# Modulation rows summed in PSUM banks, spread over two up groups and six down stages, and twelve more seven-product tiles

## What is computed

```
c_act = silu(c)
for i in range(2):
    mod = c_act @ ada_w[i] + ada_b[i]            # 1024 x 9216 weights per layer
    sh1, sc1, g1, sh2, sc2, g2, sh3, sc3, g3 = split(mod, 9)
    h = rms_norm(x, ln_ffn1[i]) * (1 + sc1) + sh1
    x = x + 0.5 * g1 * ((silu(h @ wg) * (h @ wu)) @ wd)      # 1024 -> 2816 -> 1024
    h = rms_norm(x, ln_mix[i]) * (1 + sc2) + sh2
    x = x + g2 * mixer_i(h)        # layer 0: differential attention, layer 1: spatial gating
    h = rms_norm(x, ln_ffn2[i]) * (1 + sc3) + sh3
    x = x + 0.5 * g3 * ((silu(h @ wg) * (h @ wu)) @ wd)
    x = rms_norm(x, ln_out[i])
```

## Time and profile before

| | |
|---|---|
| median of three runs | 2543.78 us (2543.47 to 2543.96) |
| the profiled execution, its own time | 2543.58 us |
| its span in the trace | 2541.7 us |
| PE busy | 2500.6 us, 98% of the span |
| DVE busy | 1466.4 us, 58% |
| ACT, POOL busy | 1109.9 and 1112.6 us, 44% each |
| chain that ended last | PE 92%, DVE 4%, DMA 1%, ACT 1%, issue 1% |
| step DMAs (512 KB) | 128 |

### The profile page before, as it was taken

One profiled execution on the slowest core, in us unless ns is written; L12 is line 12 of the kernel. 1 busy time (PEld: TensorE's weight loads), 2 busy tenths in 40 slices (PEclk: granted clock), 3 DMA queues, 4 the chain that ended last, 5 costly groups with the idle time before them and its releaser, 6 DMA issues.

```text
span 2541.7 us, 36310 instructions
## 1 busy us (share of the span) xinstructions
PE 2500.6 (98%) x14578; PEld 2182.6 (86%) x14578; DVE 1466.4 (58%) x2045; ACT 1109.9 (44%) x1933; POOL 1112.6 (44%) x578
## 2 busy tenths in 40 slices
PE   6999999999999999999999999999999999999999
PEld 5888888776888989889998988999988888889998
DVE  6767674445577635767455258453566555564543
ACT  3222224565523635425445335454554444434544
POOL 2455444232446655456564435565640000455553
PEclk8999999999999999999999999999999999999999
DMA  8687754221372333543323322333232221223322
GB/s 297 223 274 244 244 195 129 67 67 50 116 243 90 115 100 96 180 139 100 114 86 100 118 83 67 117 100 133 92 101 86 67 67 50 92 92 114 103 84 83
DMA packets 249244, 312.52 MB, mean 123 GB/s; under 512 B 7356, under 2 KB 227149, under 8 KB 248950
## 3 DMA queue, kind: packets, MB, share of 16 engines
q1 hardware_dynamic: 246762, 308.88, 36.9%
q10 hardware_dynamic: 2316, 1.33, 0.2%
HBM read 308.07 MB, written 4.74 MB: 123 GB/s over the span
## 4 chain that ended last, share of the span: by engine, by line
PE 92%; DVE 4%; DMA 1%; issue 1%; ACT 1%; POOL 0%; SPq 0%; DVEq 0%; ACTq 0%
PE bank L2320 12%; PE bank L2325 12%; PE bank L2321 12%; PE bank L2377 8%; PE bank L2380 8%; PE bank L2378 8%; PE bank L2337 6%; PE bank L2338 5%; PE bank L2342 5%; PE bank L2303 2%; PE bank L2305 1%; PE bank L2304 1%; PE bank L2392 1%; PE bank L2393 1%; PE bank L2394 1%
## 5 line engine op out<-in xcount | busy, mean ns | idle before, releaser
L937 POOL TENSOR_TENSOR w_lo_t<-w_raw,w_hi_t 128x1024 fp32r<-128x1024 f32 (+1 forms) x284 | 713.9, 2531 | 1163.4 <-ACT w_hi_t L1110 1162.9
L1110 ACT CAST w_hi_t<-w_raw 128x1024 fp32r<-128x1024 f32 (+1 forms) x316 | 311.1, 1026 | 368.5 <-PE bank L2325 175.7
L931 POOL TENSOR_TENSOR w_lo_t<-w_raw,w_hi_t 128x512 fp32r<-128x512 f32 x232 | 323.3, 1409 | 240.3 <-ACT w_hi_t L1123 238.1
L2320 PE MATMUL bank<-act_hi,w_hi_t 128*128 128x512 f32 x720 | 280.9, 390 | 1.5 <-DVE x L2025 1.3
L2320 PE MATMUL bank<-h_hi,w_hi_t 128*128 128x512 f32 x720 | 281.3, 391 | 0.6 <-ACT hidden L1377 0.6
L2321 PE MATMUL bank<-act_lo,w_hi_t 128*128 128x512 f32 x720 | 280.2, 389 | 0.0
L2321 PE MATMUL bank<-h_lo,w_hi_t 128*128 128x512 f32 x720 | 280.2, 389 | 0.0
L1681 DVE SCALAR_TENSOR_TENSOR scr<-scr,cact 128x1024 f32<-128x1024 f32 x112 | 215.0, 1920 | 62.8 <-DMA scr<-in_ada_w 54.8
L2377 PE MATMUL bank<-t_hi_t,w_hi_t 128*128 128x256 f32 x928 | 232.8, 283 | 0.0
L2378 PE MATMUL bank<-t_lo_t,w_hi_t 128*128 128x256 f32 x928 | 232.7, 283 | 0.0
L2025 DVE SCALAR_TENSOR_TENSOR x<-bank,half,x 128x512 f32<-128x512 f32 x88 | 65.9, 749 | 222.8 <-PE bank L2325 152.5
(11 more groups left out here) (316 smaller groups left out, 5727.3 us busy)
## 6 DMA issues: line engine op xcount, KB each, us to landing
scr<-in_ada_w SPq DMA_DIRECT2D x128, 512.0 KB, 6.1
w_raw<-in_ffn_wg SPq DMA_DIRECT2D x44, 1024.0 KB, 5.4
w_raw<-in_ffn_wu SPq DMA_DIRECT2D x44, 1024.0 KB, 5.3
w_raw<-in_ffn_wd SPq DMA_DIRECT2D x32, 1024.0 KB, 5.3
w_raw<-in_mlp_w SPq DMA_DIRECT2D x32, 1024.0 KB, 5.3
w_raw<-in_hgrn_w_in SPq DMA_DIRECT2D x16, 1024.0 KB, 5.4
w_raw<-in_ffn_wd SPq DMA_DIRECT2D x16, 768.0 KB, 4.4
w_raw<-in_attn_w_qkv SPq DMA_DIRECT2D x12, 1024.0 KB, 5.1
```

What stands on the lines that cost most here:

```text
L931: nc.gpsimd.tensor_tensor(piece(w_lo_q, t, j), raw_quarter(t, n, k), piece(w_hi_q, t, j).bitcast(F32), ALU.subtract).then_inc(w_lo, 1)
L937: nc.gpsimd.tensor_tensor(w_rows(w_lo_t, t, k.start, k.stop), w_raw[:, t % 2, k], w_rows(w_hi_t, t, k.start, k.stop).bitcast(F32), ALU.sub ...
L1110: act.copy(w_rows(w_hi_t, t, k.start, k.stop), w_raw[:, slot, k]).then_inc(w_hi, 1)
L2320: pe.matmul(dst, w, blk(m_hi, kb), start=kb == 0, stop=False)
```

## The change

1. The accumulator of a step moves to two PSUM banks of 512 columns: (4, 7) under the first up group, (4, 5) under the second, (2, 3) under the down stages. A step is now two DVE instructions of 512 columns, the eighth writes back into the ring buffer, and the transposed copy goes to `sq`. The ring itself moves to the columns that the activation's block sums use, with waits on `t_ok`.
2. The steps are spread anew: 24 and 8 in the first two up groups, 16 in each of six down stages (two of each of three FFNs). In a down stage DVE takes 3, 3, 2, 2, 2, 2, 1, 1 of them behind the eight updates of x. SP sends 2 behind the first weight tile, then 4, 4 and 3 behind the others and 3 between the first two tiles of the next group.
3. `std` falls: layer 0's first FFN (8, 8, 0), its second (4, 0, 0), layer 1's first (6, 0, 0). These are 12 tiles more in seven products, 70 for 58. The activation's block sums are made in the second up group of the first FFN and in the first up group of the others, no longer in down stages (except in the last MLP).
4. The PE sums of finished groups (`ada_sums`) stand behind the first two units of a down stage instead of at the end of an up group, in eight batches for five; the stage with the end of layer 0's rows and the start of layer 1's has two batches. PE waits for `ada_red` before it writes banks that held an accumulator.
5. In a group that makes the activation's sums, ACT casts three of them behind the two Silus instead of ahead.

```diff
-            ffn(layer, "ffn1", 0, (24, 24, 16), down_ada=(12, 12, 0))
+            ffn(layer, "ffn1", 0, (24, 8, 0), (8, 8, 0), down_ada=(16, 16, 0))
...
-            ffn(layer, "ffn1", 0, (16, 0, 0), (8, 0, 0))
+            ffn(layer, "ffn1", 0, (0, 0, 0), (6, 0, 0), down_ada=(16, 16, 0))
...
-            ffn(layer, "ffn2", 2, (24, 0, 0), (8, 0, 0))
+            ffn(layer, "ffn2", 2, (0, 0, 0), (4, 0, 0), down_ada=(16, 16, 0))
...
+DOWN_ROWS = (0, 3, 6, 8, 10, 12, 14, 15, 16)
+DOWN_SENT = (0, 2, 6, 10, 13, 16)
...
                 if s >= 4:
-                    sp.wait_ge(ada_ch, s - 3)
+                    if s % 8 == 3:
+                        sp.wait_ge(ada_red, (s - 3) // 8)
+                    sp.wait_ge(ada_ch, 2 * (s - 3))
...
                             weight(s, op.t0 + 2 * i + s, w[:, :, bass.ds(i * 2 * TW + (col + s * TW), TW)], kb)
                             if op.ada:
-                                for nb in ((), (0, 1), (2, 3), (4, 5, 6, 7))[2 * i + s]:
-                                    for step in down_steps(op, nb):
-                                        ada_step(step)
+                                if i == s == 0:
+                                    sp.wait_ge(x_upd, op.x0)
+                                    if staged:
+                                        sp.wait_ge(t_ok, 4 * staged)
+                                k0, k1 = DOWN_SENT[2 * i + s], DOWN_SENT[2 * i + s + 1]
+                                for step in range(op.c0 + k0, op.c0 + k1):
+                                    ada_step(step)
...
+                        for b in range(2):
+
+                            act.wait_ge(blk_mm, 4 * i + (2 * (op.t0 + 1) + b + 1))
+                            act.activation(blk(hidden, 4 + (2 * i + b) % 4), ps[b][:], ACT.Silu).then_inc(act1, 1)
+                        if i == 0 and op.makes:
                             for n in range(3):
                                 cast_t(op.stage, n)
...
+                for hf in range(2):
+                    part, acc = src[:, hf * S:(hf + 1) * S], ps[banks[hf]][:]
+                    if kb == 0:
+                        ins_ = dve.tensor_scalar(acc, part, cact[:, kb:kb + 1], None, ALU.mult)
+                    else:
+                        dve.wait_ge(ada_ch, 2 * (s - 1) + hf + 1)
+                        ins_ = dve.scalar_tensor_tensor(acc if kb < 7 else part, part, cact[:, kb:kb + 1], acc,
+                                                        ALU.mult, ALU.add)
+                    ins_.then_inc(ada_ch, 1)
...
+                                for fin in op.fins:
+                                    if fin.count > 2:
+                                        ada_sums(fin)
```

More of the change, by code:

```diff
@@ L113, in __init__ @@
         self.early, self.then, self.groups, self.std = early, None, None, std
-        self.stage, self.turns = 0, False
+        self.stage, self.turns, self.makes, self.fins = 0, False, False, []
+class Fin:
+    def __init__(self, count, groups):
+        self.count, self.groups = count, groups
+        self.layer, m = ada_block(groups[0])
+        self.m0, self.m1 = DB * m, DB * (m + len(groups))
+        self.slot = groups[0] if groups[0] < 6 else groups[0] % 2
+        self.bank = 6 if groups[0] == 0 else 1
 def ada_block(g):
@@ L229, in make_plan @@
         if op.kind in ("up", "upsq"):
-            if op.std < op.nb:
-                if op.std or last_std:
+            op.makes = 0 < op.std < op.nb or op.std == op.nb and op.t0 == 12
+            if op.makes:
+                stage += 1
+                op.stage = stage
+            elif op.std < op.nb:
+                if last_std:
                     stage += 1
-                    before.turns = not op.std
+                    before.turns = True
                 op.stage = stage
-            last_std = op.std == op.nb
+            last_std = op.std == op.nb and not op.makes
         before = op
@@ L841, in _, with pair @@
                     first = op.t0 == 0
-                    def pair(i):
+                    def pair(i, between=()):
                         weight(0, op.t0 + 2 * i, wg[:, :, bass.ds(i * TW + op.col, TW)])
+                        for step in between:
+                            ada_step(step)
                         weight(1, op.t0 + 2 * i + 1, wu[:, :, bass.ds(i * TW + op.col, TW)])
                     if not first:
-                        pair(0)
+                        pair(0, owed)
+                    owed = ()
                     for i in range(op.nb // 2):
                         steps = ada_steps(op, i) if op.ada else ()
-                        if op.ada and op.col == i == 0 and not first:
-                            sp.wait_ge(x_upd, norm_x0)
+                        if op.makes and steps and i == 2:
+                            sp.wait_ge(t_ok, 4 * op.stage)
                         for s in steps[:RING - 1]:
@@ L2043, in _ @@
                             piece_low(after.t0, 6)
+                        for step in down_steps(op, nb) if op.ada else ():
+                            ada_step(step, (2, 3))
                         if op.last and nb:
@@ L2558, in _ @@
             first_sums(ada_b_acc, 8, 8).then_inc(ada_mm, 1)
-            norm, npre, last_up = None, 0, None
-            for op in ops:
+            norm, npre, last_up, rows = None, 0, None, 0
+            for op, after in zip(ops, ops[1:] + [None]):
                 if op.kind == "norm":
@@ L2615, in _ @@
                                 unit(ps[2 * s + b][:], t, b, h_hi, h_lo, tile=None if b else t,
-                                     sums=op if op.ada and s == b == 1 and i == op.nb // 2 - 1 else None)
+                                     sums=after.fins[0] if op.ada and op.t0 == 0 and s == b == 1 and i == op.nb // 2 - 1 else None)
                 elif op.kind == "upsq":
```

125 lines of the change are left out of this document (65 added, 60 removed).

## The result

| | before | after |
|---|---|---|
| median | 2543.65 us (2543.47 to 2543.96) | 2565.43 us (2562.45 to 2569.6), four runs each |
| profiled execution, its own time | 2543.58 | 2564.65 |
| its span | 2541.7 | 2562.8 |

The ratio is 1.0087, with a 95% interval of 1.0074 to 1.0100. I had forecast 2539.2, from 2535 to 2546. Rival B, at 2550.4, was the only one that named a loss clear of noise; rival C, 2543 to 2547, at most touched one. No rival came near 22 us.

A forecast was written before the change was run, and what follows sets the result against it. PE, busy 98% of the span, was taken as the bound. Terms -9.6 - 1.1 + 1.5 + 3.7 - 1.0 + 1.0 - 0.7 + 0.6 + 1.1 = -4.5 us gave 2539.2 us, range 2535 to 2546.

The forecast's parts named there:

- Rival B: Third weight tile of all six down stages lands slower, after 8.7 us: +6.8 on the whole, 2550.4 us; chance 9%.
- rival C: DVE late with block sums of a group's second seven-product tile: 1 to 2 us in four groups, 2543 to 2547; 7%.
- The tiles: Twelve more seven-product tiles in the up groups, each saving 0.80 us: -9.6 us.
- The issue of the third tile: SP issues a down stage's third weight tile at T+13.7 in quiet stages, T+14.8 in the first one.
- The wait at 289.63: PE's 1.13 us wait for DVE's update of x goes, as steps on DVE get shorter: -1.1 us.
- The sums' departure from two down stages: Activation's sums leave two down stages that took 44.08 where a plain one takes 43.55: -1.0 us.
- The second batch's wait for `mod_ok`: First FFN's last down stage: PE waits before its second batch of sums, nearly all idle: +1.1 us.
- That is 6.7, which I take: Third weight tile in quiet down stages lands 6.7 us after issue; five stages lose +1.5 us, between 0 and 11.5.
- At nothing I cost ... the last step of a row in a stage ahead of seven-product tiles: DVE's 1.4 + 2.5 us between the first and second tile's block sums, ending 7.5 us into the first: no cost.
- The first down stage: Two bias DMAs delay its third weight tile to T+23.8, PE 3.0 late: +3.7 us for the stage.
- Sums in the up groups: Activation's sums in three more up groups: +1.0 us; Silus ahead of casts at 1550: -0.7 us.
- PE sums: Eight batches of PE sums for five, 0.2 us each: +0.6 us.

The follow-up runs named there:

- the run with six fewer: weights first with the third group of the first FFN standard again, undoing 6 of 12 new seven-product tiles: 2545.33 us.
- the fitted one: weights first plus, in five later down stages, two DVE steps before the first update and none after the last; thirteenth step sent earlier, old Silu order in two groups: 2535.49 us.
- weights first: Changed kernel with only SP's order altered: third and fourth weight tiles behind the fourth step, next group's two behind the eighth and twelfth: 2541.07 us.
- the first experiment: The same run as weights first: only SP's sending order altered against the changed kernel, 2541.07 us.
- both edits: Changed kernel with SP's order of weights first and DVE taking four steps ahead of a down stage's first update: 2556.63 us.
- refitted: both edits with SP's order fitted to DVE's: fourth weight tile behind the sixth step instead of the fourth: 2555.64 us.
- next group's tiles only: Changed kernel with the next group's first tile right behind the fourth tile, its second ahead of the last three steps; third tile unmoved: 2563.05 us.
- last row's turn left out: Changed kernel with the transposition and reduction of each down stage's last row replaced by one copy of 32 columns: 2561.77 us.
- bias DMAs later: Changed kernel with all eight bias DMAs behind the fourth weight tile of the first down stage: 2566.35 us.
- steps early: Changed kernel with only DVE's order altered: four steps ahead of a down stage's first update, none behind the last: 2542.60 us.

## Why the prediction was wrong

**Where the 21.1 us between the spans lie,** by stages from start to start: first down stage +5.5 (49.16 for 43.68); the four other down stages with rows and a seven-product group behind them +6.0 after 44.08, 43.55, 44.07 and 43.55 in before; the one from 272.52 -0.3; the seven-product groups +11.4 (the four that were there) and -2.2 (the new one, where -5.1 was to be had); the groups that make the activation's sums -1.8, -0.5 and +0.4; the three last down stages +2.4; the start +0.9; the rest together -0.7.

**Right.** The tiles: 0.80 each, shown by the run with six fewer. The issue of the third tile: I had T+13.7 and T+14.8, measured T+13.6 and T+14.9. The wait at 289.63 is gone, although its stage fell by only 0.3 us in the changed kernel, as the late third tile took its place; in the fitted one it fell by 1.1 (43.96 for 45.08). The sums' departure from two down stages gives 0.53 each (43.54 in the fitted order for 44.08). The second batch's wait for `mod_ok` is 0.95 us, forecast 1.1 with its sums.

**The step that failed first: "That is 6.7, which I take".** The third tile landed after 7.6, 8.7, 7.7, 7.6 and 8.1 us in the five quiet stages. I had set the two rows aside that said 7.4 and 8.7, because their queue had been busy; the idle queue here gave nothing. The conversion that I gave, 1.0 us lost at 7.4 and 2.3 at 8.7, holds roughly: the stage that landed after 8.7 took 46.03, 2.5 over 43.55, and those with 7.6 to 8.1 lost 1.3 to 1.8, of which 0.4 to 0.5 in three of them is the PE sums of a batch (the fitted kernel's 43.96, 44.07 and 43.98). The five together lost 8.3, some 6.9 without these sums, where I had 1.5. That is rival B's mechanism, at about 9%.

Both terms of the 6.7 were too small. The step just ahead of the tile landed 4.5 to 5.3 us after the tile's issue, for 4.1, and the tile 2.9 to 3.4 after that, for 2.6. My 410 GB/s came from a microsecond with four steps and a weight tile in flight, and not steps alone. Here the queue took until 1285 to come near it:

```profile
1281.00:1282.00 1.00, 1.00 (x6) 0.84 (x5) 0.90 (x4) 0.00 (x0) 0.00 (x0) 1.00 0.82 242
1282.00:1283.00 1.00, 1.00 (x6) 0.82 (x5) 1.00 (x3) 0.00 (x0) 0.00 (x0) 1.00 0.87 303
1283.00:1284.00 1.00, 1.00 (x6) 0.83 (x5) 1.00 (x2) 0.00 (x0) 0.00 (x0) 1.00 0.97 312
```

The next step leaves 0.9 us after the tile and lands 1.3 after it, so one might blame the DMAs issued behind. Other tiles speak against that. In before, the one issued at 187.53 had nothing ahead of it in flight and four steps behind it from 0.5 us on, and landed like one alone:

```profile
187.53 0.38 SPq L769 DMA_DIRECT2D w_raw<-in_ffn_wu  x1
188.00 2.39 SPq L778 DMA_DIRECT2D scr<-in_ada_w  x4
...
DMA to landing us min/median/max: 5.3/5.3/5.3
```

With one step 0.4 us ahead a tile took 6.1 us with nothing behind it (before, 200.77) and 6.3 with three steps behind it from 0.9 on (weights first, 907.30). With two steps 1.8 and 0.4 us ahead and nothing behind it took 7.4 and 7.9 (before, 221.27 and 701.53; an older step was still to land there). So what tells here is how much is still in flight ahead; beside 7.4 and 7.9, the 7.6 to 8.7 leave 0.8 us at most for what stands behind. Why the queue ran below 410 GB/s in those microseconds stays open.

The sentence from the Trainium skill (DMA: Bandwidth & Descriptors, "Anatomy of one DMA"), by whose figure the landings would, as an estimate, have come 0.8 us earlier, pointed away from the measurement here: its time is that of one DMA, and none of these moved alone.

**The step that failed most: "At nothing I cost ... the last step of a row in a stage ahead of seven-product tiles".** I computed the third tile and stopped. SP's queue went on: the fourth tile and the next group's two stood behind the same waits, 14, 14 and 9 us later than before. My figure for the end of the row, 7.5 us into the first tile, took DVE's work alone; it ended at 9.4 in the stage followed above, where DVE had stood 3.6 us idle for a tile that SP had not sent in time. The price was 14.3 us in five groups. Rival C named this place, with 1 to 2 us in four groups and DVE's load as the reason. The place was right, the size was 1.9 to 3.8 in five, and the reason was mostly the queue on SP: in the first experiment DVE does the same work in the same order, and 10.3 of the 14.3 us are gone.

**The first down stage** was forecast at +3.7 and lost 5.5. PE's wait was 3.66, for 3.0 forecast. Most of the rest is its clock. The windows behind the wait (PEclk is the third column from the right):

```profile
160.00:162.00 2.00, 0.00 (x0) 0.03 (x1) 0.00 (x0) 1.19 (x2) 0.07 (x1) 1.00 1.04 413
162.00:163.50 1.50, 1.50 (x6) 1.21 (x7) 1.46 (x3) 0.81 (x1) 1.50 (x1) 0.96 1.02 408
163.50:166.50 3.00, 3.00 (x8) 2.31 (x7) 2.93 (x4) 0.00 (x0) 3.00 (x2) 0.50 1.03 395
166.50:168.00 1.50, 1.50 (x7) 1.27 (x6) 1.50 (x3) 0.00 (x0) 0.18 (x1) 0.90 1.08 385
```

PE restarted at full speed for 1.5 us. Then for 3 us the granted clock was 0.50, the lower level (1.2 GHz), and a matmul took 0.43 us in place of 0.23: some 1.5 us more. In the FFNs of before no wait was longer than the 1.13 us of the earlier trace rows, so its trace could not show this.

**Sums in the up groups.** I had +1.0 and -0.7. Against their tiles' pace the three groups take 1.7, 1.4 and 1.7 us more, and the one at 1550 had taken 1.3: 3.5 in place of 0.3. The reorder gained nothing at 1550; its wait moved to the turn, 1.05 us behind the same Silus, which the waits above show as L1397.

**PE sums.** I had 0.2 us for a batch. The fitted kernel's down stages with one batch take 0.4 to 0.5 us over the plain 43.55, so the three more cost some 1.3 in place of 0.6.

**The start.** +0.9 that no part of the change explains: PE's clock was raised at about 50.7 us in the changed kernel's trace and at 48.3 in before's, with the same instructions ahead of it. The same stretch took 12.3 to 13.9 us over all the runs here.

**The chances.** Slower had 7%. The reason given for the low figure was that the queue has been idle for several microseconds. That held for its first DMA only: in the quiet stages the first step landed after 3.5 to 3.7 us, as alone, the second already after 4.9 to 5.7.

## What to carry to other kernels

When transfers are moved ahead of others in an in-order queue, follow the queue until it is back on its old times, not only to the first item that is late; here moving the tile that I computed gave 17 us of 24, and moving those behind it as well gave the rest. Two in-order queues that feed each other (a ring's sender and its consumer) are one schedule: each of two edits was worth over 20 us alone, and together they gave 9. Take a landing time from the row with the same DMAs in flight ahead of it, and do not set such a row aside for a reason that no row shows.

## What the runs showed of the hardware

- After 3.66 us without a matmul TensorE ran 1.5 us at full speed and then 3 us at the lower of its two clocks. Its matmuls also went to 0.43 us after the waits of 2.64 (both edits), 3.20 (refitted), 3.92 (next group's tiles only) and 4.43 us (last row's turn left out) in the first down stage, for 2.5 to 3.5 us, and after the one of 3.03 behind it (bias DMAs later) for some 5.5 us. They kept their pace after the one of 2.73 (steps early): the length of the wait alone does not tell.
- A 1 MB tile landed 5.2 us after its issue alone, 5.3 with four steps behind it, 6.1 to 6.3 with one step 0.4 us ahead, and 7.4 to 8.7 with two steps in flight ahead. The first down stage's third and fourth tile, beside the DRAM copies of the bias, took 9.5 and 12.7 in the changed kernel, and the tile behind all eight copies 11.4.
- The half step on a PSUM accumulator took 0.73 to 0.76 us in all 256 cases (in 32 of them the result goes back to SBUF), the first of a group (a multiplication with its operand in SBUF) 0.744 to 0.754: no case of the 3.4 us that the full step in SBUF had the earlier trace rows. The taken value, 0.75, was right.
